# Other settling matmuls, a triangular sum of a pair in one matmul, and index queries turned earlier, in a two-layer decoder trunk

## The reference

```
layer 0:  x += stick_breaking_attention(rmsnorm(x))      16 heads of 128
          x += conv_ffn(rmsnorm(x))                      d_ff 5632
layer 1:  x += sparse_attention(rmsnorm(x))
          x += conv_ffn(rmsnorm(x))

stick breaking:  z = q k^T / sqrt(128);  s = softplus(z), 0 where key >= query
                 between = reverse_cumsum_over_keys(s) - s
                 a = exp(log_sigmoid(z) - between);  out = a v
sparse:          index score = sum over 16 heads of relu(rope(qi) ki^T) * wi
                 the 64 highest keys of each token are kept, softmax over them
conv_ffn:        u = h w_up;  c = depthwise causal conv of width 3 over u
                 out = (silu(gate half of c) * value half of c) w_down
```

## Time and profile before

| | |
|---|---|
| median of three runs | 2255.68 us (2255.61 to 2256.72) |
| the profiled execution's own time | 2255.47 us |
| its span in the trace | 2253.7 us |
| PE busy | 2240.5 us (99%), 13143 matmuls |
| DVE busy | 1497.0 us (66%) |
| ACT busy | 1167.9 us (52%) |
| granted PE clock | full in all 40 slices |

### The profile page before, as it was taken

How to read it: one execution, slowest core, us unless ns; L and a number is a source line. 1 busy time by engine, 2 the same in 40 slices (tenths; PEclk the granted TensorE clock), 3 DMA queues, 4 the chain that set the end, 5 groups by cost and what they waited for, 6 DMA issues and landing times.

```text
span 2253.7 us, 36186 instructions
## 1 busy us (share of the span) xinstructions
PE 2240.5 (99%) x13143; PEld 1973.6 (88%) x13143; DVE 1497.0 (66%) x1778; ACT 1167.9 (52%) x1400; POOL 2.5 (0%) x9
## 2 busy tenths in 40 slices
PE   9999999999999999999999999999999999999999
PEld 8999998888888888888889888888888888888888
DVE  7655556677777777545577887667777777774444
ACT  7555545555555555444454455555555555554332
POOL 0000000000000000000000000000000000000000
PEclk9999999999999999999999999999999999999999
DMA  7545455555555555555556544465655555556654
GB/s 258 169 160 172 158 168 187 187 186 182 187 189 181 184 186 192 186 185 186 186 194 197 181 147 143 136 195 175 201 181 196 182 197 186 188 187 205 200 194 139
DMA packets 113537, 411.97 MB, mean 183 GB/s; under 512 B 12736, under 2 KB 13376, under 8 KB 113472
## 3 DMA queue, kind: packets, MB, share of 16 engines
q1 hardware_dynamic: 112464, 407.49, 54.6%
q10 hardware_dynamic: 576, 1.97, 0.2%
q0 software_dynamic: 432, 1.57, 0.2%
HBM read 408.88 MB, written 2.10 MB: 182 GB/s over the span
## 4 chain that ended last, share of the span: by engine, by line
PE 90%; DVE 6%; issue 1%; ACT 1%; DMA 0%; DVEq 0%; ACTq 0%
PE psum L1024 90%; DVE w_lo L584 2%; ACT w_hi L261 1%; DVE rb L807 1%; ACT pr L480 0%; DVE rb L793 0%; DVE tu L785 0%; DVE ra L811 0%; DVE tu L783 0%; DVE mx L887 0%; DVE score L839 0%; DVE ra L805 0%; DVE xg L599 0%; DMA vecs<-vecs_in 0%; DVE pr L899 0%
## 5 line engine op out<-in xcount | busy, mean ns | idle before, releaser
L584 DVE TENSOR_TENSOR w_lo<-raw,w_hi 128x1024 fp32r<-128x1024 f32 x772 | 938.2, 1224 | 699.8 <-ACT w_hi L261 694.1
L1024 PE MATMUL psum<-xg,w_hi 128*128 128x512 f32 (+1 forms) x3936 | 1369.8, 394 | 2.8 <-DVE xg L599 2.8
L261 ACT CAST w_hi<-raw 128x1024 fp32r<-128x1024 f32 x772 | 804.3, 1050 | 801.2 <-PE psum L1024 797.0
L1024 PE MATMUL psum<-xg,w_lo 128*128 128x256 f32 (+1 forms) x3936 | 1094.9, 278 | 0.0
L1024 PEld LDWEIGHTS psum<-xg,w_hi 128*128 128x128 f32 x3936 | 738.1, 188 | 166.3 <-issue 2.2
L1024 PEld LDWEIGHTS psum<-xg,w_lo 128*128 128x128 f32 x3936 | 743.9, 189 | 2.4 <-issue 2.2
L1024 PE MATMUL psum<-hid,w_hi 128*128 128x512 f32 x1408 | 492.9, 395 | 0.0
L1024 PE MATMUL psum<-hid,w_lo 128*128 128x256 f32 x1408 | 394.8, 280 | 0.0
L1024 PEld LDWEIGHTS psum<-hid,w_hi 128*128 128x128 f32 x1408 | 263.9, 187 | 62.0
L1024 PEld LDWEIGHTS psum<-hid,w_lo 128*128 128x128 f32 x1408 | 266.0, 189 | 0.0
L1024 PE MATMUL psum<-att,w_hi 128*128 128x512 f32 x512 | 178.8, 394 | 0.0
(11 more groups left out here) (152 smaller groups left out, 914.6 us busy)
## 6 DMA issues: line engine op xcount, KB each, us to landing
raw<-w_all SPq DMA_DIRECT2D x772, 512.0 KB, 3.3
xres<-x_in SPq DMA_DIRECT2D x4, 512.0 KB, 7.3
cst<-consts_in ACTq DMA_DIRECT2D x2, 768.0 KB, 4.7
out_t<-xres POOLq DMA_DIRECT2D x3, 512.0 KB, 3.5
out_t<-xres SPq DMA_DIRECT2D x4, 128.0 KB, 1.8
vecs<-vecs_in ACTq DMA_DIRECT2D x1, 354.0 KB, 6.4
avg_d<-consts_in SPq DMA_DIRECT2D x1, 64.0 KB, 9.3
vecs<-vecs_in ACTq DMA_DIRECT2D x1, 32.0 KB, 4.3
```

The costliest lines, as they stand in the source:

```text
L261: act.copy(w_hi[:, c % RING, :], raw[:, c % RING, :]).then_inc(hi_ready, 1)
L584: dve.tensor_tensor(w_lo[:, c % RING, :], raw[:, c % RING, :], f32(w_hi[:, c % RING, :]), ALU.subtract).then_inc(lo_ready, 1)
L1024: return pe.matmul(o, lhsT, rhs, start=start, stop=True, skip_group_check=True)
```

## The change

Four edits. `settle` alternates: a matmul of 256 columns ahead of each one of 128, six in all. `settle(4)` behind the last `l0_av` is gone. `l0_tri` takes the late keys of both heads, which lie side by side, in one matmul of 256 columns in place of two of 128. On DVE the rotary step of the index queries moves to the head of the block, ahead of split 0, the scores move behind split 1, and `select(1)` moves from behind split 0 to behind split 2 of its block.

```diff
@@ block1 on DVE
+                    if e == 0 and prev is not None and prev[0] == "qi":
+                        rope_prev(B - 1, *prev)
                     split(base + e + RING, i, per)
-                    if e == 0 and t_score is not None:
+                    if e == 1 and t_score is not None:
                         add_scores(t_score)
-                    if e == 1 and prev is not None:
+                    if e == 1 and prev is not None and prev[0] != "qi":
                         rope_prev(B - 1, *prev)
...
             def topk_c(e):
-                if e == 0:
+                if e == 2:
                     select(1)
...
             def settle(bank):
                 for n in range(3):
+                    mm(psum[:, bank, 0:T], xg[:, 0, 0:P], xg[:, 1, 0:T], True)
                     mm(psum[:, bank, 0:P], xg[:, 0, 0:P], xg[:, 1, 0:P], True)
...
-                    for h in range(2):
-                        last = mm(psum[:, 6, h * P:(h + 1) * P], tri_r[:, :], sp_hl[:, part_, Z1 + h * P:Z1 + (h + 1) * P])
+                    last = mm(psum[:, 6, 0:T], tri_r[:, :], sp_hl[:, part_, Z1:ZN])
                 last.then_inc(la_ready, 1)
...
                 if e == 3:
                     l0_av(PAIRS - 1)
-                    settle(4)
```

## The result

The changed kernel takes 2235.1 us in the median of four executions (2234.61 to 2236.73), the kernel before beside it 2256.2. The ratio of the first comparison is 0.9893, with a 95% interval of 0.9863 to 0.9922. The eight times listed for it don't give that ratio: their medians give 0.9907, and the lowest over the highest 0.9901. Two later comparisons with more executions give 0.9909 (0.9892 to 0.9925) and 0.9909 (0.9897 to 0.9922). The change is faster by 0.9%. The forecast was 2235.9 us in a range of 2233.5 to 2252.0. The two later ratios give 2235.2.

What follows compares the result with a forecast made beforehand. PE, busy 2240.5 us of a 2253.7 us span, was taken to bound the kernel. Terms of -5.8 us, with layer 0's pace -19.6 us, took 2255.47 us to 2235.9 us; range 2233.5 to 2252.0.

Steps and rivals of the forecast that it cites:

- the two paces: PE's matmul pairs in the MLPs: 353.3 ns a pair in layer 0, 346.7 ns in layer 1, with nothing waited for.
- Layer 0's pace: Layer 0's MLP stretch: the new settle leaves PE at the better pace, -13.8 us, bounds 0 and -13.8.
- Layer 1's pace: Layer 1's MLP stretch: already at the better pace and keeps it, 0 us; +13.7 us if lost.
- `settle`: Behind the statistic in each layer: the added matmuls lie on PE's path, +0.3 us a layer, +0.6 us.
- `settle(4)` removed: Behind the last l0_av: three matmuls of 128 columns go, -0.4 us; 1.8 us lost if the better pace goes.
- `l0_tri`: Eight places in the loop: one matmul of 256 for two of 128, -1.6 us, ends -0.7 to -2.5 us.
- The index stage: Index blocks of layer 1: PE's wait for qr goes, 0.74 us each for six, -4.4 us, bounds -3.0 and -4.6.
- the likeliest case: Both MLP stretches at the better pace and the wait gone: 2235.9 us, own range 2234 to 2240, chance 0.46.
- layer 0 gains nothing: Rival: layer 0's MLP keeps the worse pace and layer 1's the better, 2249.7 us, chance 0.20.
- the paces swap: Rival: layer 0's MLP gains the better pace and layer 1's loses it, 2249.6 us, chance 0.16.
- The slower case (both worse): Rival: the new settle leaves PE at the worse pace in both MLPs, 2263.4 us, chance 0.16.
- The index wait: Rival: in the index blocks splits come late for PE in place of qr, 4.4 us given back, 2240.3 us, chance 0.02.

Runs made afterwards that it cites:

- the kernel with the added couple: The change plus one couple (matmuls of 256 and 128 columns) ahead of layer 1's output projection: 2235.51 us in four executions, later 2236.87 us in six.
- the one with three of 256: The kernel with the added couple, its settle(5) made three matmuls of 256 columns and none of 128: 2263.66 us in one execution.

## Why the prediction was right or wrong

**What bounds, and the two paces: right.** The gain is in PE's pace, -13.8 us of -18.8, in the very stretch and of the size named. The view that showed it was the count of matmuls in equal windows.

**Layer 0's pace: right in size, the reason half right.** The couples suffice, as the new settle alone showed (2242.9 us, expected 2242.6). They weren't needed here: with the other edits PE comes in even, and the old settle does as well (4040 matmuls in 700 us). The prediction had the pace set by the short matmuls of the statistic and of `settle`, counted nothing for the removed `settle(4)` beyond its own time, and mentioned only what losing the pace behind it would cost. Together with `l0_tri` the removal changed how PE comes into the statistic, and that alone is worth the 13.8 us as well. Either way was enough; the forecast counted one, and the size came out right.

**Layer 1's pace: right.** 3925 matmuls in 680 us before and after. Here the couples were put to a harder test than I had thought, since PE came in slow in the profiled execution. But the old settle passed that one too. The entry that it fails from, the uneven one, came up at layer 1 in the two traces of the kernel with the added couple, and the new settle left at the better pace both times.

**`settle`: right.** +0.35 us a layer against +0.3. **`settle(4)` removed: right** for its own time, within 0.1 us (0.33 us by its own starts).

**`l0_tri`: mis-sized, the step that failed.** The term was -1.6 us, with a lower end of -2.5, and it measured -2.5. The duration as such was right; the timeline, for the earlier trace rows:

```profile
50.96 0.28 PE L1026 MATMUL psum<-xg,w_lo 128*128 128x256 f32 x1
51.08 0.40 PE L1026 MATMUL psum<-sp_hl,tri_r 128*128 128x512 f32 x1
...
52.27 0.28 PE L1026 MATMUL psum<-xg,w_lo 128*128 128x256 f32 x1
...
57.47 0.28 PE L1026 MATMUL psum<-xg,w_lo 128*128 128x256 f32 x1
```

52.27 - 50.96 = 1.31 us, where 1.28 to 1.32 was forecast. What the sum left out, and named only as a bound, is the pace of the pairs behind: 15 pairs in 57.47 - 52.27 = 5.20 us, 346.7 ns, where it had been 354. That is 0.1 us each time, 0.9 us in all. The k pieces behind kept theirs. The prediction named this gain and an equal loss in the k pieces as the ends of the term and put neither into the sum. With the measured term the forecast is 2235.0 us, against a median of 2235.1.

**The index stage: right.** 4.4 us, and from the last matmul of a block to the next block's first the same 1.23 us every time, as here, for the earlier trace rows:

```profile
1198.68 0.25 PE L1026 MATMUL psum<-xg,w_lo 128*128 128x192 f32 x1
1198.77 1.50 PE L1026 MATMUL psum<-ki,qr 128*128 128x128 f32 x8
1199.91 0.52 PE L1026 MATMUL psum<-xg,w_hi 128*128 128x384 f32 x1
```

DVE's order in the loop, for the earlier trace rows:

```profile
1190.77 0.55 DVE L779 TENSOR_TENSOR tu<-psum,tu 128x384 f32<-128x384 f32 x1
1191.36 0.56 DVE L791 TENSOR_TENSOR ra<-tu,cst 128x384 f32<-128x384 f32 x1
1191.93 1.12 DVE L793 TENSOR_TENSOR rb<-tu,cst 64x384 f32<-64x384 f32 x2
1193.17 0.56 DVE L799 TENSOR_TENSOR qr<-ra,rb 128x384 f32<-128x384 f32 x1
1193.65 1.22 DVE L584 TENSOR_TENSOR w_lo<-raw,w_hi 128x1024 fp32r<-128x1024 f32 x1
1195.51 1.23 DVE L584 TENSOR_TENSOR w_lo<-raw,w_hi 128x1024 fp32r<-128x1024 f32 x1 [0.64 <-ACT w_hi L261]
```

`qr` stands 2.4 us behind `tu` and five microseconds ahead of PE's logits at 1198.8. DVE still waits for ACT ahead of the second split, and PE's list of waits has none for `w_lo`, so no split is late for PE.

**`select(1)`: right**, at nothing.

**Not in the sum: +1.6 us.** The output projection of layer 1 fell to the slow pace in the profiled execution. The prediction priced this at +1.8 in its range for the likeliest case, but not as something that differs from one execution to the next. With both misses, -0.9 and +1.6, the forecast gives 2236.6 us for such an execution, and the profiled one took 2236.73. The two have opposite signs, so that the forecast of 2235.9 lies between the two groups of executions is in part luck. The median of 2235.1 belongs to the lower group, where the trace of 2235.07 us has the projection at the better pace.

**The range.** Its lower end was 2233.5 us. The ends named for the likeliest case give 2235.0 to 2240.9 us, where 2234 to 2240 was written, so below the forecast there was little but the 0.9 us of `l0_tri`. The 0.2% (4.5 us) that the prediction took as the least that a measurement can tell was used for the line between faster and same, and the range got none of it. The first ratio's interval, 0.9863 to 0.9922, reaches from 2225 to 2238 us on its own. Its middle, 2231.5 us, isn't borne out: no execution of the change was under 2234.6 us, no term measured so much, and the later ratios give 2235.2. What made the first ratio so low isn't known.

**The rivals.** That layer 0 gains nothing or that the paces swap was refuted by the windows, 4040 and 3925 matmuls. The reason given for the former, that three couples fade into whatever phase PE brings along, is refuted by the new `settle` alone, which left the uneven entry at the better pace where the old one left it slow. The slower case (both worse) didn't come, but it is real: the kernel without a settle and the one with three of 256 are there, at 2262.9 and 2263.7 us against the 2263.4 of that rival. The index wait did not move: the list of waits shows no new one.

## What to carry to other kernels

Where one engine is busy 99% of the time, count its instructions in equal windows of like work: the count shows a pace that busy time, waits and the granted clock all hide. A long run of like matmuls kept the arrangement that it began with here, over 730 us. So price an edit ahead of such a run by the run's length too, and look in which arrangement PE comes in: two edits that gave 0.3 and 2.5 us by themselves were together worth 13.8 us behind them. When a term is taken at its middle, ask whether the rows next to it, here the pairs behind `l0_tri`, change with it. Take several executions before believing half a per cent, and look whether they lie in groups.

## What the runs showed of the hardware

- The same pairs of fp32r matmuls (512 and 256 columns, each with its own weight load) run in three repeating arrangements, all at the full granted clock and with no wait: starts 346 to 347 ns apart, 350 and 343 in turn, or 350, 361 and 349 in turn. The last is 1.9% slower and lasted 730 us (2.1 thousand pairs) without leaving.
- Which one follows a float32 statistic went with the short matmuls behind it and the arrangement ahead of it, without an exception in 30 places (the table above; some of its cells hold one). Why 256 and 128 columns in turn, three times, take all three to a better pace isn't known; no run took the phase itself apart.
- Behind a wait of PE the float32 logits took 1.22 us to the next piece, without it 1.14. A wait listed as 0.5 us cost 0.74 us.
